# Gate tiles 2 to 7 of a hybrid decoder layer by seven block products instead of eight

## What is computed

```python
h = rmsnorm(x, norm_mix)
proj = h @ w_in + b_in                       # conv_val, conv_gate, pool_in, gate_a, gate_b: 1024 columns each
u = conv_val * sigmoid(conv_gate)
u = silu(layernorm(causal_dwconv(u, 31 taps)))
ya = u @ conv_w_out
yb = pool_branch(pool_in)                    # trailing means over 2, 4, 8, 16 positions, minus the token, four small maps
merged = sigmoid(gate_a) * ya + sigmoid(gate_b) * yb
x = x + merged @ mix_w_out
x = x + gdfn(rmsnorm(x, norm_ffn))           # up to 2 x 2816, conv of 3, gelu(a) * b, down
return rmsnorm(x, norm_final)
```

## Time and profile before

| | us |
|---|---|
| median of 3 runs | 1312.87 |
| lowest, highest | 1312.77, 1314.28 |
| the profiled execution's own time | 1312.89 |
| its span in the trace | 1311.1 |
| PE busy in the span | 1295.5 |

### The profile page before, as it was taken

One profiled execution on the slowest core, in us unless ns is written; L12 is line 12 of the kernel. 1 busy time (PEld: TensorE's weight loads), 2 busy tenths in 40 slices (PEclk: granted clock), 3 DMA queues, 4 the chain that ended last, 5 costly groups with the idle time before them and its releaser, 6 DMA issues.

```text
span 1311.1 us, 15929 instructions
## 1 busy us (share of the span) xinstructions
PE 1295.5 (99%) x5886; PEld 1077.0 (82%) x5886; DVE 935.8 (71%) x1066; ACT 425.7 (32%) x596; POOL 812.2 (62%) x529
## 2 busy tenths in 40 slices
PE   8999999999999999999999999999999999999997
PEld 7888888888888888888888788888888888888887
DVE  5898989999584533334768666776667678877975
ACT  6211221211113460011216343433434346333551
POOL 4536636454544353356856888788788876567761
PEclk9999999999999999999999999999999999999999
DMA  9211101110111112334422323322322339877923
GB/s 345 82 32 48 49 32 48 49 49 32 48 48 48 49 48 81 110 122 144 144 73 73 112 98 120 113 88 89 121 104 89 120 124 389 305 273 261 371 98 129
DMA packets 55700, 156.16 MB, mean 119 GB/s; under 512 B 4432, under 2 KB 12624, under 8 KB 51920
## 3 DMA queue, kind: packets, MB, share of 16 engines
q1 hardware_dynamic: 51952, 145.80, 31.3%
q10 hardware_dynamic: 3680, 9.44, 2.0%
HBM read 126.65 MB, written 28.57 MB: 118 GB/s over the span
## 4 chain that ended last, share of the span: by engine, by line
PE 91%; DVE 4%; ACT 2%; issue 1%; POOL 1%; DMA 1%; SPq 0%; DVEq 0%; ACTq 0%; POOLq 0%
PE ps L1674 30%; PE ps L1676 30%; PE ps L1675 30%; DVE tmp L1379 1%; DMA cv<-in_x 1%; PE ps L1738 0%; ACT cv L823 0%; PE ps L1728 0%; ACT cv_r L1025 0%; POOL w_lo L749 0%; DVE res L1459 0%; DVE res L1490 0%; DVE res L1431 0%; DVE cv L1370 0%; POOL h_lo L708 0%
## 5 line engine op out<-in xcount | busy, mean ns | idle before, releaser
L1674 PE MATMUL ps<-h_lo,w_hi 128*128 128x512 f32 (+1 forms) x972 | 376.2, 387 | 1.9 <-DVE h_lo L1237 1.9
L1675 PE MATMUL ps<-h_hi,w_lo 128*128 128x512 f32 (+1 forms) x972 | 374.3, 385 | 0.0
L1676 PE MATMUL ps<-h_hi,w_hi 128*128 128x512 f32 (+1 forms) x972 | 374.3, 385 | 0.0
L663 POOL TENSOR_SCALAR w_hi<-raw 128x1024 fp32r<-128x1024 f32 x62 | 68.6, 1106 | 288.2 <-issue 241.7
L1674 PEld LDWEIGHTS ps<-h_lo,w_hi 128*128 128x128 f32 x972 | 182.7, 188 | 39.6 <-DVE h_lo L1237 3.1
L1675 PEld LDWEIGHTS ps<-h_hi,w_lo 128*128 128x128 f32 x972 | 182.7, 188 | 36.4 <-issue 0.2
L1676 PEld LDWEIGHTS ps<-h_hi,w_hi 128*128 128x128 f32 x972 | 182.6, 188 | 36.4
L1317 DVE SCALAR_TENSOR_TENSOR ps<-tmp,par,ps 128x512 f32<-128x512 f32 x224 | 158.2, 748 | 0.0
L665 POOL TENSOR_TENSOR w_lo<-raw,w_hi 128x1024 fp32r<-128x1024 f32 x62 | 154.2, 2487 | 5.2
L1674 PE MATMUL ps<-ga_r,w_hi 128*128 128x512 f32 (+1 forms) x383 | 149.1, 389 | 2.5 <-DVE res L1528 2.1
L1675 PE MATMUL ps<-cv_r,w_lo 128*128 128x512 f32 (+1 forms) x383 | 148.4, 388 | 0.0
(11 more groups left out here) (231 smaller groups left out, 2252.4 us busy)
## 6 DMA issues: line engine op xcount, KB each, us to landing
raw<-in_wstream SPq DMA_DIRECT2D x68, 512.0 KB, 3.4
tmp<-in_wffn SPq DMA_DIRECT2D x13, 1024.0 KB, 4.8
g_kept<-res SPq DMA_DIRECT2D x21, 512.0 KB, 2.8
res<-in_wffn SPq DMA_DIRECT2D x10, 1024.0 KB, 4.8
ga_r<-g_kept SPq DMA_DIRECT2D x18, 512.0 KB, 7.1
h_lo<-g_kept SPq DMA_DIRECT2D x17, 512.0 KB, 6.5
g_kept<-raw SPq DMA_DIRECT2D x12, 512.0 KB, 2.8
tmp<-in_wffn SPq DMA_DIRECT2D x6, 704.0 KB, 5.6
```

The costliest lines, as they stand in the source:

```text
L663: pool.tensor_scalar(hi, r, 1.0, 0.0, ALU.mult, ALU.add).then_inc(w_hi_done, 1)
L1674: nc.tensor.matmul(out, a_hi, b_lo, start=start, stop=False, skip_group_check=onto)
L1675: nc.tensor.matmul(out, a_lo, b_hi, start=False, stop=False, skip_group_check=onto)
L1676: return nc.tensor.matmul(out, a_hi, b_hi, start=False, stop=stop, skip_group_check=onto)
```

## The change

`START` now ends with a0 v7 g7 a1. For c = 2 to 7, gates a and b of tile c form a pair g = c - 2, whose two chunks W11 W12 and W21 W22 are two output tiles by two halves of the input channels. Instead of 8 block products of 12 matmuls, PE makes 7 (`gate_product`), in the order W11*B11, S2*T2, S1*T1, S3*T3, W12*B21, W22*T4, S4*B22.

The four sums T of the normed input take the place of `res` (and their high parts that of `ga`). The second halves of the normed input are written to DRAM early and loaded back; the first halves are put together from high and low part by POOL (`b`), which also makes the first sum (`t`). The other three sums and four low parts of T are DVE's, the four high parts ACT's. So the pooled branch and gates 0 and 1 go to DRAM first, every later gate and pooled tile follows it there through the unused halves of `h_hi`, and all come back while the last pair runs. The high parts of the weights move from POOL to ACT, 512 columns at a time; POOL makes four sums and seven low parts a pair. The multiplication of gate b onto the pooled branch moves from POOL to DVE. The five sums of the products are DVE's too. For pairs 0 and 1 they stand inside `conv(7)`, between its taps, and from pair 2 on between the steps of the layer norm, as its ACT and PE steps do on those engines.

```diff
 START = tuple((x[0], int(x[1])) for x in (
-    "v0 g0 v1 g1 p0 p1 v2 g2 p2 p3 m0 v3 g3 p4 p5 m1 v4 g4 p6 p7 v5 g5 m2 b0 b1 v6 g6 m3 a0 a1 v7 g7").split())
+    "v0 g0 v1 g1 p0 p1 v2 g2 p2 p3 m0 v3 g3 p4 p5 m1 v4 g4 p6 p7 v5 g5 m2 b0 b1 v6 g6 m3 a0 v7 g7 a1").split())
...
+GP = KT - PAIR0
+GATE_OPS = NP7 * GP
+FIRST_GATE = CHUNK["a", PAIR0]
...
-    BESIDE.setdefault(N_PAIRS + 2 * _c + 3, []).append(f"gb{_c}")
+          23: ["gb1"], 25: ["glu6", "cs4", "b0"], 26: ["cs5", "b1"], 27: ["t0"]}
+
...
+        def gate_bank(g, i):
+
+            return bank((0, 1, 7, 2, 3)[(3 * g + i) % 5])
+
...
+            for name, k in (("T3", 0), ("T2", 4)):
+                sp.dma_start(t_place(res, name), norm_dram[:, k:k + 4, :]).then_inc(norm_kept, 16)
+            load_gates(0)
+            sp.wait_ge(s1_out, out_of(TURN["a", 1]))
+            sp.dma_start(a_dram[:, 0:2, :], tiles(ga, 0, 2)).then_inc(a_kept, 16)
+            sp.wait_ge(a_kept, 16)
+            load_pooled(PAIR0)
+            for c in range(PAIR0, KT - 1):
+                load_gates(c - PAIR0 + 1)
+                if c == KT - 2:
...
+                    sp.wait_ge(a_kept, gates_kept(k0)[0])
+                    sp.wait_ge(y_kept, gates_kept(k0)[1])
+                sp.dma_start(tiles(ga, k0, k1), a_dram[:, k0:k1, :]).then_inc(a_kept, 16)
+                sp.dma_start(tiles(res, k0, k1), y_dram[:, k0:k1, :]).then_inc(a_kept, 16)
+            load_chunks(N_OUT // 2 + 1, NCHUNKS // 2)
             o_d = outT.rearrange("(k p) n -> p k n", p=P)
             def ffn_weights(b, dst, n):
 
...
+                if what == "b":
+                    name, k = (("T1", 0), ("T4", 4))[i]
+                    pool.wait_ge(y_kept, 16 * NG)
+                    pool.tensor_tensor(t_place(res, name), four(h_hi, k, 0).bitcast(f32), four(h_lo, k, 0).bitcast(f32),
+                                       ALU.add).then_inc(t_sum, 1)
...
+                    pool.wait_ge(t_sum, 1)
+                    pool.tensor_tensor(t_place(res, "T1"), t_place(res, "T1"), t_place(res, "T3"), ALU.subtract).then_inc(t_sum, 1)
...
                     wait(pool, pool_mm, 2 * i)
...
+            for g in range(GP):
+                w11, w12, w21, w22 = gate_w
+                s1, s2 = gate_sums(g)
+                gate_low(g, P1, w11)
+                pool.wait_ge(raw_loaded[1], 16 * (FIRST_GATE // 2 + g + 1))
+                wait(pool, f_wlo, NP7 * g)
+                if g == 0:
+                    pool.wait_ge(gb_done, PAIR0)
+                pool.tensor_tensor(s1, w21, w22, ALU.add).then_inc(f_sum, 1)
+                pool.wait_ge(f_sum, 4 * g + 1)
+                pool.tensor_tensor(s2, s1, w11, ALU.add).then_inc(f_sum, 1)
+                pool.wait_ge(f_sum, 4 * g + 2)
+                gate_low(g, P6, s2)
+                if g == 0:
+                    beside("glu", KT - 1)
+                    beside("cs", KT - 2)
+                gate_low(g, P5, s1)
+                pool.tensor_tensor(w21, w11, w21, ALU.add).then_inc(f_sum, 1)
+                pool.wait_ge(f_sum, 4 * g + 3)
+                gate_low(g, P7, w21)
+                gate_low(g, P2, w12)
+                pool.wait_ge(f_wlo, NP7 * g + P5 + 1)
+                pool.tensor_tensor(s1, s2, w12, ALU.add).then_inc(f_sum, 1)
+                gate_low(g, P4, w22)
+                pool.wait_ge(f_sum, 4 * g + 4)
+                gate_low(g, P3, s1)
+
+            pool.sem_inc(w_split, 2 * GP)
+            pool.sem_inc(w_hi_done, 2 * GP)
+            for s, j in ((0, P2), (1, P3)):
+                pool.wait_ge(raw_loaded[s], 16 * (N_OUT // 2 + 1))
...
+            act.dma_start(norm_dram, res[:, :].rearrange("p (k n) -> p k n", k=KT)[:, :, HALF:SEQ]).then_inc(norm_kept, 16)
...
+            turn, n = TURN[LAST_PLAIN], CHUNK[LAST_PLAIN]
+            gate_t("T1", 3)
+            gate_high(0, P1)
+            for h in range(2):
+                act.wait_ge(*((s1_half, turn + 1) if h == 0 else (w_used, n + 1)))
+                act.activation(tile(ga, 1, *span(h)), slot(1, *span(h)), ACT.Sigmoid, bias=par1("b_in", 3 * KT + 1)).then_inc(s1_out, 1)
+                if h == 0:
+                    gate_t("T3", 4)
+                    gate_t("T2", 5)
+                    gate_high(0, P6)
+            gate_high(0, P5)
+            gate_high(0, P7)
+            for g in range(2):
+                gate_first(g)
+                gate_high(g, P2)
+                if g == 0:
+                    gate_t("T4", 6)
+                gate_high(g, P4)
+                gate_high(g, P3)
+                gate_a1(g)
+                gate_b_half(g, 1)
+                gate_high(g + 1, P1)
+                gate_b_half(g, 0)
+                gate_high(g + 1, P6)
+                gate_high(g + 1, P5)
+                gate_a2(g)
+                gate_high(g + 1, P7)
+
...
+                c = PAIR0 + g
+                dve.wait_ge(f_v1, g + 1)
+                dve.wait_ge(f_used, NP7 * g + P6 + 1)
+                if PAIR0 < c < KT - 1:
+                    dve.wait_ge(a_kept, gates_kept(c - 1)[0])
...
+
...
+
+                dve.wait_ge(f_used, NP7 * g + P7 + 1)
...
+                dve.tensor_tensor(sgb_half[1], gate_bank(g, 1), gate_v1[g % 2], ALU.subtract).then_inc(f_post, 1)
+                dve.wait_ge(f_post, gate_posted(g, "u3"))
+                dve.tensor_tensor(sgb_half[1], sgb_half[1], gate_bank(g, 2), ALU.subtract).then_inc(f_post, 1)
...
+            dve.wait_ge(t_sum, 3)
+            t1, t2, t3, t4 = (t_place(res, name) for name in ("T1", "T2", "T3", "T4"))
+            dve.tensor_tensor(t3, t3, t2, ALU.subtract).then_inc(t_sum, 1)
+            dve.wait_ge(t_sum, 4)
+            dve.tensor_tensor(t2, t1, t2, ALU.add).then_inc(t_sum, 1)
+            dve.wait_ge(t_sum, 5)
+            dve.tensor_tensor(t4, t4, t2, ALU.subtract).then_inc(t_sum, 1)
+            gate_t_low("T2", 3)
+            gate_t_low("T1", 1)
+            gate_t_low("T3", 2)
+            gate_u2(0)
+            gate_t_low("T4", 4)
+
+            def last_of(g):
+                gate_c12(g)
+                gate_pooled(g)
+
+            conv(KT - 1, {1: lambda: gate_c22(0), 3: lambda: gate_c21(0), 5: lambda: last_of(0), 7: lambda: gate_u2(1),
+                          9: lambda: gate_c22(1), 11: lambda: gate_c21(1), 12: lambda: last_of(1), 14: lambda: gate_u2(2)})
 
...
+            centre(0, 1)
+            gate_c21(2)
+            centre(2)
+            add_square(0)
+            last_of(2)
+            centre(3)
+            add_square(1)
+            centre(4)
+            add_square(2)
+            gate_u2(3)
+            centre(5)
+            add_square(3)
+            centre(6)
+            add_square(4)
+            gate_c22(3)
+            centre(7)
+            add_square(5, 6, 7)
+            gate_c21(3)
...
+            for g in range(GP):
+                if g == 0:
+                    pe.wait_ge(val_out, KT - 1)
+                elif g == 1:
+                    pe.wait_ge(s1_out, out_of(TURN[LAST_PLAIN]))
+                else:
+                    pe.wait_ge(f_post, gate_posted(g - 2, "c21"))
+                gate_product(g, P1, 0, True)
+                if g == 4:
+                    variance(slot(3), [((ln["sum"], KT), csum)], var_done, KT)
+                if g == 0:
+                    pe.wait_ge(t_lo, 1)
+                elif g >= 2:
+                    pe.wait_ge(f_post, gate_posted(g - 2, "c12"))
+                gate_product(g, P6, 1, True)
+                if g == 0:
+                    pe.wait_ge(t_lo, 2)
+                else:
+                    pe.wait_ge(s1_out, gates_read(g - 1, 1))
+                gate_product(g, P5, 2, True)
+                if g == 4:
+                    broadcast(ln, slot(2), 16)
+                if g == 0:
+                    pe.wait_ge(t_lo, 3)
+                pe.wait_ge(f_post, gate_posted(g, "u2"))
+                gate_product(g, P7, 1, False)
+                pe.wait_ge(f_v1, g + 1)
+                gate_product(g, P2, 0, False)
+                if g == 2:
+                    for h in range(2):
+                        mean_of(slot(2, *span(h)), csum[:, h * HALF:(h + 1) * HALF], (cs_done, KT), ln["mean"])
+                if g == 0:
+                    pe.wait_ge(t_lo, 4)
+                pe.wait_ge(f_post, gate_posted(g, "u3"))
+                gate_product(g, P4, 1, False)
+                pe.wait_ge(f_post, gate_posted(g, "c22"))
+                gate_product(g, P3, 2, False)
+            pe.sem_inc(w_used, 2 * GP)
 
 
             def pairs(first_n, free, read_out, mov_hi, mov_lo, ready, last_half=None):
@@ -1883,7 +2335,8 @@
```

459 lines of the change are left out of this document (339 added, 120 removed).

## The result

| | before | changed |
|---|---|---|
| median of the runs, us | 1312.82 | 1326.76 |
| lowest to highest, us | 1312.72 to 1314.28 | 1325.39 to 1328.76 |
| ratio, 95% interval | | 1.0105, 1.0087 to 1.0122 |
| profiled execution, span / own time, us | 1311.1 / 1312.89 | 1327.0 / 1328.76 |

The changed kernel is slower by 1.05%. Its profiled execution, from which all rows of the changed kernel come, is the slowest of its four, 2.0 us above the median.

A forecast was written before the change was run, and what follows sets the result against it. PE was taken as the bound, as long as its feed keeps up: -16.3 for removed matmuls, +15.1 first pair, +4.3 pairs 1 and 2, +4.3 pair 3, +1.7 the rest, +9.1 in all, giving 1322.0 us; range 1306 to 1332.

The forecast's parts named there:

- the forecast's own case: Whole kernel: 1314 to 1326 us around the forecast of 1322.0, chance 0.57.
- Turns on the shared port: DVE instructions with both inputs in SBUF and POOL instructions exclude each other and alternate; DVE's T instructions take 3.4, not 2.28.
- The first pair: Pair 0: PE stalls 3.8 at S2*T2, 8.9 at S1*T1, 0.5 at S3*T3, 1.9 at W22*T4; sum 15.1 us.
- Pairs 1 and 2: DVE is the bound: PE waits 2.5 us for u2 of pair 1 and 1.8 at the mean.
- Pair 3: In the layer norm, DVE's centres and square additions delay u2 by 3.4 and u3 by 0.9: 4.3 us.
- Pairs 4, 5 and the hand-over: Low part of S2 0.9, gate a of pair 4 0.4, gate b of tile 7 0.4: 1.7 us.
- The clock: Half clock after the first pair's long stall: S1*T1 2.7 us longer, mostly covered; 0 to 2.7 on the sum.
- the 8.9 us stall: First pair: PE waits 8.9 us before S1*T1 for POOL's low part of S1.
- no wait in this trace is long enough to show it in the middle: PE in the trace before the change: no mid-kernel wait long enough to show idleness dropping the clock; longest 2.1 us.
- Side by side: Rival: DVE's sums and low parts of T and POOL's work do not delay each other; 1309 us, chance 0.20.
- The norm breaks the pairs further: Rival: four more square additions meeting POOL on PE's path in the layer norm cost 8.8; 1331 us, chance 0.17.
- That the changed products work as in the feed-forward part: Rival: gate products are fed as in the feed-forward part, nearly all of 16.3 us stays; 1297 us, chance 0.06.

The follow-up runs named there:

- the run with one operand in PSUM: Changed kernel with low parts of T1 and T3 made by four 512-column subtractions reading one operand from PSUM (wrong values, rows only): 1324.57 us, single run.
- The pieces of 512: Third replanned kernel with DVE's two-SBUF-operand instructions in the stage cut into 512-column pieces, plus some reordering: 1326.71 us, ratio 1.0090.
- the first run above: Changed kernel with 12 and 27 dummy matmuls in PE's two waits of pair 0, for the low parts of T2 and S1: 1326.92 us, ratio 1.0104.
- The run with the shift moved: Changed kernel with the two-place shift of the weights' slots moved from pair 3's first product to its fourth: 1326.22 us, ratio 1.0091.
- four plans: Changed kernel reordered, with the norm's PE steps behind products of pairs 3 and 4, in four successive versions: 1322.70, 1318.54, 1318.53 and 1326.71 us.

## Why the prediction was right

The median, 1326.76 us, lies in the range of 1306 to 1332 and 4.8 above the forecast of 1322.0, 0.8 above the end of the forecast's own case (1314 to 1326).

**Turns on the shared port: right.** The rows of T's sums, 3.27 us against 3.4 foreseen, the low parts (10.83 for three), the glu, and above all the run with one operand in PSUM show it. The Trainium skill, "SBUF — State Buffer", section "Who interferes with whom", has the second instruction fully blocked until the first ends. The pieces of 512 agree with it, 1.75 for 1.3 + 0.6 less the overlap at the start.

**The first pair: right, 1.3 us too dear.** Foreseen starts 351.6, 363.2 and 373.8 for S2*T2, S1*T1 and W22*T4, measured 350.80, 361.96 and 372.46: 13.8 of the 15.1 us. The idle times in the rows, 2.9 and 6.6, are below the 3 to 5 and 7 to 10 foreseen; the second because S2*T2 before it ran at the lower level and took 1.7 of that stop. That the end of the pair is set by W22*T4's operands, which cover the clock, is shown by the first run above.

**Pairs 1 and 2: right for u2, not for the mean.** u2 of pair 1 cost 2.5 us, as foreseen. The mean wasn't waited for (1.8 foreseen). DVE had its input ready at 415.60, as foreseen (415.5 to 416.7), but PE came at 415.65 and not at 414.3: 1.7 us by the clock, 0.6 for POOL, less the 1.1 that it was early at u2. The 0.6, in pair 2, was not in the forecast.

**Pair 3: the size about right, the cause wrong.** 4.3 us foreseen for u2 and u3 behind the norm's additions; measured 3.2, all of it for the low part of S2. u2 was out in time. The step that failed is that DVE's list would be last: ACT's high part of W11 was, because it went to a slot that had been used two products before. The run with the shift moved shows it.

**Pairs 4, 5 and the hand-over: too small.** 1.7 foreseen, 4.8 measured: gate a of pair 4 behind eight silus and a table load cost 3.2 and not 0.4, gate b of tile 7 1.6 and not 0.4; the 0.9 for the low part of S2 in pair 4 didn't come.

**The clock: the mis-sized term.** Foreseen at 0, or 2.7 at the upper end. In the first pair it was covered. But the prediction looked for it only behind the 8.9 us stall; behind waits of 2.3, 3.0 and 3.0 us the clock fell too, with less to cover it: 1.7 + 1.7 + 3.0 = 6.4 us of running matmuls in the profiled execution. (Of the first 1.7 DVE and POOL would have covered a part: in the first run above, without that stretch, the mean starts 1.1 us earlier.) The step "no wait in this trace is long enough to show it in the middle" was true of the trace and no bound. The Trainium skill, "TensorE: Matmul & The Clock Gate", section "The HAM clock gate", says that idleness drops the array to 1.2 GHz until it has been busy again. These rows agree in that each of the five stretches begins in a wait or within 1.0 us behind one, but not every wait brings one (the last section).

Together: -16.3 + 13.8 + 2.5 + 0.6 + 3.2 + 4.8 + 6.4 = +15.0, measured 14.9 at the projection and 15.9 at the end of the profiled execution; at the median 13.9, where the forecast had 9.1. Without the clock the measured terms make +8.6, near the forecast, but that is luck in part: pairs 0 to 3 came out 3.6 us cheaper than foreseen, and pairs 4, 5 and the hand-over 3.1 us dearer.

**The rivals.** Side by side is excluded by the rows. "The norm breaks the pairs further" didn't come about as told: from pair 3 on PE waited for none of DVE's steps. That the changed products work as in the feed-forward part wasn't reached by order either: the two best of four plans got from +13.9 to +3 and +4 us (ratios 1.0024 and 1.0033), none below the kernel before.

**What stays open.** Whether a better order would win isn't shown. And what the three later lower-level stretches cost in the median isn't either, since dummies in those waits moved nothing: the profiled executions say 3 us at the projection, the times and ratios say 1 at most. That the lower level costs time at all in the unprofiled executions is suggested by their own clocks: of the changed kernel's four, the two with a mean granted clock of 0.992 took 1325.4 and 1325.8 us, the two with 0.989 1327.8 and 1328.8; of the kernel before, beside the experiments, 21 executions with 0.998 took 1312.6 to 1313.4 us, and 8 with 0.994 1316.3 to 1317.2. The two go together; which brings the other these numbers can't say.
